# Weighted sums of an attention with the values as the stationary operand, turned back to token rows in the output projection, and sums of squares of the delta norm taken by ACT

## What is computed

```python
def stick_breaking_attention(q, k, v):      # 8 heads of 64
    for blk in range(seq // SB_BLOCK):      # 8 row blocks of 128 tokens
        logits = einsum('bhtd,bhsd->bhts', qh[:, :, start:end], kh[:, :, :end])
        log_remain = where(causal, log_sigmoid(-logits), 0.0)
        log_after = cumsum(log_remain, axis=3, reverse=True) - log_remain
        weights = where(causal, exp(log_sigmoid(logits) + log_after), 0.0)
        outs.append(einsum('bhts,bhsd->bhtd', weights, vh[:, :, :end]))

# in gated_deltanet, o is (seq, 4 heads, 128)
o = rms_norm(o, norm_w) * silu(zf)
# in reference
sb_out = rms_norm(stick_breaking_attention(sb_q, sb_k, sb_v), sb_norm_w[i])
mixed = concatenate([gdn_out, sb_out], axis=-1)
x = x + einsum('bsc,cd->bsd', mixed, w_out[i])
```

## Time and profile before

| | before |
|---|---|
| median of 3 runs | 1545.11 us (1543.13 to 1546.72) |
| the profiled execution | 1548.61 us |
| its span, first to last instruction | 1546.6 us |
| PE busy over the span | 1383.3 us (89%) |
| DVE, ACT, POOL busy | 553.6, 358.9, 257.5 us |
| granted PE clock, mean over the span | 0.957 |
| mixers, from PE's first to its last multiplication | 451.5 to 694.2 us of the span |
| output projection, PE's first transposes to the last route and embed work | 695.3 to about 856 us |

### The profile page before, as it was taken

How to read it: one execution, slowest core, us unless ns; L and a number is a source line. 1 busy time by engine, 2 the same in 40 slices (tenths; PEclk the granted TensorE clock), 3 DMA queues, 4 the chain that set the end, 5 groups by cost and what they waited for, 6 DMA issues and landing times. The chain is left out here.

```text
span 1546.6 us, 16490 instructions
## 1 busy us (share of the span) xinstructions
PE 1383.3 (89%) x5986; PEld 743.0 (48%) x5986; DVE 553.6 (36%) x847; ACT 358.9 (23%) x674; POOL 257.5 (17%) x372
## 2 busy tenths in 40 slices
PE   6999999999999999999999687788778878789997
PEld 4445864444458878874555232232223323234443
DVE  3323024432227887872455221211211111124543
ACT  2221132100036666651212101000000100004322
POOL 1000000110014544532110111111111111111110
PEclk8999999999999999999999899999989999999999
DMA  5212025743422220106214499999999999982231
GB/s 195 68 68 69 14 70 170 196 116 89 141 104 62 65 73 28 29 8 272 81 63 150 173 411 420 421 420 417 418 411 399 404 403 403 402 368 91 82 122 41
DMA packets 107879, 306.96 MB, mean 198 GB/s; under 512 B 22560, under 2 KB 61360, under 8 KB 82096
## 3 DMA queue, kind: packets, MB, share of 16 engines
q1 hardware_dynamic: 98032, 289.42, 49.0%
q0 software_dynamic: 9792, 16.80, 2.9%
HBM read 285.16 MB, written 39.90 MB: 210 GB/s over the span
## 5 line engine op out<-in xcount | busy, mean ns | idle before, releaser
L1620 PE MATMUL pe_gu<-w_gu,xT 128*64 128x512 f32 x1024 | 266.8, 681 | 97.1 <-DMA w_gu<-in_w_expert_up 91.2
L251 PE MATMUL ps<-wide,gst 128*128 128x512 f32 x640 | 285.7, 607 | 3.2 <-DVE wide L404 3.2
L1620 PEld LDWEIGHTS pe_gu<-w_gu,xT 128*64 128x64 f32 x1024 | 82.2, 155 | 259.8 <-issue 257.9
L251 PEld LDWEIGHTS ps<-wide,gst 128*128 128x128 f32 x640 | 123.6, 195 | 155.1 <-issue 153.3
L1824 DVE TENSOR_TENSOR hs<-sg,pe_gu 128x256 f32<-128x256 f32 x32 | 13.5, 421 | 361.0 <-ACT sg L1736 361.0
L1314 PE MATMUL p_x<-wide,pw 128*128 128x512 f32 x256 | 116.4, 608 | 2.1 <-DVE mx L1174 1.4
L1638 PE MATMUL pe_y<-wide,hTe 128*64 128x512 f32 x512 | 115.4, 592 | 1.1 <-DVE ys L1829 1.1
L901 POOL TENSOR_TENSOR wt<-brk,Pm 128x512 f32<-128x512 f32 (+3 forms) x96 | 91.1, 950 | 125.1 <-DVE Pm L827 120.7
L265 PE MATMUL psk<-w_tok,wide 128*128 128x260 f32 (+1 forms) x384 | 111.7, 453 | 0.0
L1709 PE MATMUL pe_y<-w_gu,xT 128*128 128x512 f32 x256 | 111.2, 592 | 0.0
L1560 POOL DMA_INDIRECT y_d<-ys,row_at x32 | 32.5, 1017 | 425.8 <-DVE ys L1829 415.1
(11 more groups left out here) (303 smaller groups left out, 1572.7 us busy)
## 6 DMA issues: line engine op xcount, KB each, us to landing
w_gu<-in_w_expert_gate SPq DMA_DIRECT2D x64, 1024.0 KB, 11.8
w_gu<-in_w_expert_up SPq DMA_DIRECT2D x64, 1024.0 KB, 16.5
wide<-in_w_expert_down SPq DMA_DIRECT2D x64, 1024.0 KB, 19.6
gst<-in_w_in SPq DMA_DIRECT2D x20, 512.0 KB, 4.0
wide_tab<-y_d SPq DMA_DIRECT2D x8, 1024.0 KB, 5.6
qkv_d<-y_sb SPq DMA_DIRECT2D x12, 512.0 KB, 2.6
qk_st<-rows_d SPq DMA_DIRECT2D x8, 768.0 KB, 9.6
gst<-qkv_d SPq DMA_DIRECT2D x8, 768.0 KB, 4.8
```

The lines of the kernel that those rows point to most:

```text
L251: last = pe.matmul(ps[s][:, c], w_ct[:, s, k, :], hT[:, k, c], start=k == 0, stop=k == KT - 1)
L1620: last = pe.matmul(p_gu[e * CAP:(e + 1) * CAP, :], xT[:, s, k, e * CAP:(e + 1) * CAP], wv[:, e, :, k, :], start=k == 0, stop=k == KT - 1)
```

## The change

* Weighted sums: the 64 columns of the values are now the stationary operand and the turned weights (128 columns) the moving one. The two heads of a pair write the upper and the lower 64 partitions of `OB`, so that `OB` holds the result turned: head width by tokens. The sums of both strips of a pair are issued in one group, block by block and head by head, in steps g = 4, 6, 8, ...; there are 48 groups in place of 96. `wT` has a second pair of buffers. The tiles of `mx` that the attention fills are turned, too.
* Output projection: each tile's attention half is first turned back (`turn_back`, 4 transposes into the upper half of `p_m`), ACT takes the squares from there, and DVE's `norm_heads` reads `p_m` and writes the token rows. `turn_back(0)` comes first, `turn_back(1)` after `turn_s(0)` in step 0, and `turn_back(t + 1)` at the start of step t from t = 1. `turn_s` then writes the same part of `p_m`. POOL's root for the delta half of the last tile, DVE's `gated_last` and ACT's squares for them come ahead of the work on tile 1.
* Delta norm: ACT squares head by head, four instructions of 128 columns with an accumulated sum; DVE's `sum` is gone; DVE's `norm` is four instructions of 128 columns with both factors in place of two of 512.
* `scale_w_o` moves from DVE to ACT, at half steps 14 and 22.
* `nsq` and `own` have no memory of their own any more and lie in `w_r` and `ln_row`; so the router weights are loaded after the seventh squares, and `ln_row` after the last scan.
* PE's wait for the memsets stands in the first `ks` piece only.

```diff
--- before.py
+++ after.py
...
         St, Sg = sb("St", [P, GH, P]), sb("Sg", [P, GH, P])
-        nsq = sb("nsq", [P, GW])
+        nsq = w_r[:].rearrange("p k n -> p (k n)")[:, 0:GW]
         nss = sb("nss", [P, GH])
...
         wt = sb("wt", [P, 3, 512])
-        wT = sb("wT", [P, 2, 512])
-        own = sb("own", [P, 512])
+        wT = sb("wT", [P, 2, 2, 512])
+        own = ln_row[:, 0:512]
         GA, GB, GC = (pb(n, [P, GH, P]) for n in ("GA", "GB", "GC"))
...
         PE_AT = {"y1": 0, "xq": 2, "z1": 5, "vt": 7, "y2": 9, "kt": 11, "z2": 13, "ks": 15, "vn": 18, "ods": 21}
-        ACT_AT = {"y1": 0, "xq": 2, "square": 4, "y2": 9, "vn": 18}
-        DVE_AT = {"scale0": 0, "q": 1, "gain": 1, "x": 2, "v": 3, "sum": 3, "k": 5, "xT": 6, "r": 7, "scale1": 8, "norm": 9, "s": 10, "o": 11}
+        ACT_AT = {"y1": 0, "xq": 2, "square": 4, "y2": 9, "scale0": 14, "vn": 18, "scale1": 22}
+        DVE_AT = {"q": 1, "gain": 1, "x": 2, "v": 3, "k": 5, "xT": 6, "r": 7, "norm": 9, "s": 10, "o": 11}
...
                 sp.dma_start(w_o[:], A["w_out"][0].rearrange("(k p) c -> p k c", p=P)).then_inc(wo_in, 16)
-                sp.dma_start(w_r[:, :, 0:NG], A["w_router_group"][0].rearrange("(p k) c -> p k c", k=KT)).then_inc(small_in, 16)
-                sp.dma_start(w_r[:, :, NG:NG + NE], A["w_router_expert"][0].rearrange("(p k) c -> p k c", k=KT)).then_inc(small_in, 16)
                 sp.dma_start(b_r[:, 0:NG], A["b_router_group"][0:1, :].to_broadcast([P, NG])).then_inc(small_in, 16)
                 sp.dma_start(b_r[:, NG:NG + NE], A["b_router_expert"][0:1, :].to_broadcast([P, NE])).then_inc(small_in, 16)
-                sp.dma_start(ln_row[:], A["ln_moe"][0:1, :].to_broadcast([P, D])).then_inc(small_in, 16)
                 for i in range(NT - 2):
...
                     load_z(i + 2)
+                sp.wait_ge(nss_ok, NT - 1)
+                sp.dma_start(w_r[:, :, 0:NG], A["w_router_group"][0].rearrange("(p k) c -> p k c", k=KT)).then_inc(small_in, 16)
+                sp.dma_start(w_r[:, :, NG:NG + NE], A["w_router_expert"][0].rearrange("(p k) c -> p k c", k=KT)).then_inc(small_in, 16)
+                sp.wait_ge(scan_done, G)
+                sp.dma_start(ln_row[:], A["ln_moe"][0:1, :].to_broadcast([P, D])).then_inc(small_in, 16)
...
-                def weighted(g):
-
-                    t, n, c0, c1, e = at(g)
+                def weighted(m):
+
+                    g = 2 * m
+                    t, n, c0, c1, _ = at(g)
                     if g % NS == 0:
                         reach(pe, at_done, g // NS)
-                    pe.wait_ge(ev_done, g + 1)
-                    m = (c1 - c0) // P
-                    h = g // (2 * NS) * 2 + e
-                    for b in range(m):
-                        last = pe.matmul(OB[:, n, e * SD:(e + 1) * SD], wT[:, e, b * P:(b + 1) * P], v_sb[:, c0 // P + b, h * SD:(h + 1) * SD],
-                                         start=g % NS == 0 and b == 0, stop=g % NS == NS - 1 and b == m - 1)
+                    pe.wait_ge(ev_done, g + 2)
+                    nb = (c1 - c0) // P
+                    for b in range(nb):
+                        for e in range(2):
+                            h = g // (2 * NS) * 2 + e
+                            last = pe.matmul(OB[e * SD:(e + 1) * SD, n, :], v_sb[:, c0 // P + b, h * SD:(h + 1) * SD], wT[:, m % 2, e, b * P:(b + 1) * P],
+                                             start=g % NS == 0 and b == 0, stop=g % NS == NS - 2 and b == nb - 1)
                     last.then_inc(pv_done, 1)
...
                     elif piece == "ks":
+                        if i == 0:
+                            pe.wait_ge(setup, 3)
                         for h in range(GH):
...
-                pe.wait_ge(setup, 3)
                 for g in range(G + 3):
...
                         transposes(g - 2)
-                    if g >= 3:
-                        weighted(g - 3)
+                    if g >= 4 and g % 2 == 0:
+                        weighted(g // 2 - 2)
                     if g < G:
...
                     act.wait_ge(tr_done, g + 1)
-                    reach(act, pv_done, g - 1)
-                    act.activation(wT[:, e, 0:m], TB[e][:, 0:m], ACT.Copy).then_inc(ev_done, 1)
+                    reach(act, pv_done, g // 2 - 1)
+                    act.activation(wT[:, g // 2 % 2, e, 0:m], TB[e][:, 0:m], ACT.Copy).then_inc(ev_done, 1)
...
                     c = slice(GW + i // 2 * P, GW + (i // 2 + 1) * P)
-                    act.wait_ge(pv_done, (i + 1) * NS)
+                    act.wait_ge(pv_done, (i + 1) * NS // 2)
                     if i % 2 == 0:
...
+                def scale_w_o(k):
+                    act.wait_ge(wo_in, 16)
+                    act.wait_ge(nw_in, 48)
+                    last = act.activation(w_o[:, k, :], w_o[:, k, :], ACT.Copy, scale=nw[:, k // GH:k // GH + 1])
+                    if k == KT - 1:
+                        last.then_inc(wo_ok, 1)
+
                 def delta(piece, i):
+                    if piece[0:5] == "scale" and 1 <= i <= KT // 2:
+                        scale_w_o(2 * (i - 1) + int(piece[5]))
                     if piece[0] == "y":
...
                         act.wait_ge(O_ok, i)
-                        reach(act, nss_ok, i - 1)
-                        act.activation(nsq[:], mx[:, i - 1, 0:GW], ACT.Square).then_inc(nsq_ok, 1)
+                        reach(act, nm_ok, i - 1)
+                        for h in range(GH):
+                            c = slice(h * GD, (h + 1) * GD)
+                            last = act.activation(nsq[:, c], mx[:, i - 1, c], ACT.Square, accum_out=nss[:, h:h + 1])
+                        last.then_inc(nss_ok, 1)
                     elif piece == "vn":
...
-                def scale_w_o(k):
-                    dve.wait_ge(wo_in, 16)
-                    dve.wait_ge(nw_in, 48)
-                    last = dve.tensor_scalar(w_o[:, k, :], w_o[:, k, :], nw[:, k // GH:k // GH + 1], None, ALU.mult)
-                    if k == KT - 1:
-                        last.then_inc(wo_ok, 1)
-
                 def delta(piece, i):
...
                     b3 = lambda x: x.unsqueeze(2).to_broadcast([P, GH, P])
-                    if piece[0:5] == "scale" and 1 <= i <= KT // 2:
-                        scale_w_o(2 * (i - 1) + int(piece[5]))
-                    elif piece == "q":
+                    if piece == "q":
                         dve.wait_ge(qk_done, i + 1)
...
                         dve.tensor_tensor(mx[:, i, 0:GW], mx[:, i, 0:GW], GC[:].rearrange("p h n -> p (h n)"), ALU.add).then_inc(O_ok, 1)
-                    elif piece == "sum" and i > 0:
-                        dve.wait_ge(nsq_ok, i)
-                        dve.tensor_reduce(nss[:], nsq[:].rearrange("p (h n) -> p h n", h=GH), AX.X, ALU.add).then_inc(nss_ok, 1)
                     elif piece == "norm" and i > 0:
...
                         dve.wait_ge(nrs_ok, i)
-                        dve.tensor_tensor(o.rearrange("p (h n) -> p h n", h=GH), o.rearrange("p (h n) -> p h n", h=GH),
-                                          nss[:].unsqueeze(2).to_broadcast([P, GH, GD]), ALU.mult).then_inc(nz_step, 1)
-                        dve.wait_ge(nz_step, i)
                         dve.wait_ge(z_in[1 - s], 16 * ((i - 1) // 2 + 1))
-                        dve.tensor_tensor(o, o, z_sb[:, 1 - s], ALU.mult).then_inc(nm_ok, 1)
+                        for h in range(GH):
+                            c = slice(h * GD, (h + 1) * GD)
+                            last = dve.scalar_tensor_tensor(o[:, c], o[:, c], nss[:, h:h + 1], z_sb[:, 1 - s, c], ALU.mult, ALU.mult)
+                        last.then_inc(nm_ok, 1)
...
                 def step(t, s, half_t, first, last):
-                    if not last:
-                        heads_rms(t + 1, 1 - s)
                     if first:
...
                         pool.tensor_tensor(gss[:], gss[:], nh[:, 0:GH], ALU.pow).then_inc(gs_ok, 1)
+                    if not last:
+                        heads_rms(t + 1, 1 - s)
+                    if first:
                         constants()
...
                         act.wait_ge(ms_sum, nth)
-                    act.activation(msq[:, s], row(t, slice(GW, None)), ACT.Square).then_inc(msq_ok, 1)
+                    act.wait_ge(back_done, t + 1)
+                    act.activation(msq[:, s], p_m[:, HK:].rearrange("p k n -> p (k n)"), ACT.Square).then_inc(msq_ok, 1)
...
                 copy_g(0, 0)
-                head_squares(1, 1, None)
                 act.activation(hsq[:, 0:GW], row(NT - 1, slice(0, GW)), ACT.Square).then_inc(gsq_ok, 1)
                 copy_s(0, 0)
+                head_squares(1, 1, None)
                 act.wait_ge(gs_sum, 1)
...
                     dve.wait_ge(ms_ok, t + 1)
-                    dve.tensor_tensor(heads(t), heads(t), mss[:, s].unsqueeze(2).to_broadcast([P, SH, SD]), ALU.mult).then_inc(m_ok, 1)
+                    dve.wait_ge(back_done, t + 1)
```

(23 more changed lines are left out.)

6 lines of the change are left out of this document (3 added, 3 removed).

## The result

| | before | after |
|---|---|---|
| median of 14 runs each, on the same chip | 1545.92 us (1538.64 to 1552.9) | 1537.72 us (1529.4 to 1544.46) |
| ratio after to before, 95% interval | | 0.9947 (0.9925 to 0.997) |
| the profiled execution, its span | 1548.61, 1546.6 us | 1542.1, 1540.2 us |
| PE, DVE, ACT, POOL busy over the span | 1383.3, 553.6, 358.9, 257.5 us | 1371.2, 543.5, 371.2, 251.5 us |
| granted PE clock, mean | 0.957 | 0.955 |

A forecast was written before the change was run, and what follows sets the result against it. PE was taken to bound both stages. Mixers -14.9 us (-10.6 - 6.3 + 2) and output projection +10.7 us (0.3 + 5.4 + 2.6 + 2.4) gave -4.2 us: median 1545.1 to 1540.9 us; 80% range 1532 to 1553.

The forecast's parts named there:

- Streaming pair: Weighted sums in the mixers: both halves stream at the same time, 0.115 us per pair, 33.1 us for 288 pairs.
- rival 2: Weighted sums: second half's load lies bare or halves don't overlap at 128 columns; 1570 to 1574 us, chance 0.12.
- Changing the form: Mixers: entering and leaving the divided array costs 0.35 us for each of 48 groups, 16.8 us in all.
- rival 4: Weighted sums: changing the form is nearly free, 0.05 us per group, -14 us more, 1527 us; chance 0.10.
- The wait for `OB`: Mixers, start of each round: PE's 6.8 us wait for ACT's copies is covered by the later first sum, -6.3 us.
- New waits: Mixers: waits behind ACT's squares and scalings, for DVE's scan, POOL's product and PE's transpose; +2 us (0 to +8).
- rival 1: The forecast itself: halves stream together, PE stays the bound, new waits 0 to 6 us; 1535 to 1547 us, chance 0.58.
- DVE and ACT: Mixers: DVE loses about 20 us of 192, to 172; ACT gains 13 of 149, to 162; PE stays the bound.
- `ln_row`: Start of the output projection: its later load lands as PE begins, a tie; +0.3 us (0 to +1.5).
- Step 0: Output projection: PE waits for tile 1's whole chain, 6.8 us where it was 1.84; +5.4 us with 0.5 at the start.
- The clock: Output projection: after 4 us of standing still PE's clock falls again, +2.4 us (0 to +3.3).
- Later steps: Output projection: the turn backs of tiles 2 to 7 stand in full steps, 2.6 us.

The follow-up runs named there:

- e6: The changed kernel with every weighted-sum group of two or more blocks cut in two, over two steps; 1544.55 us, ratio to the kernel before 0.9991.
- e4: The kernel before with only the new delta norm and the scaling of w_o on ACT; 1549.68 us, ratio to the kernel before 1.0032.
- e3: The changed kernel with the delta norm and the scaling of w_o as they were before; 1538.24 us, ratio to the kernel before 0.9942.
- e8: The kernel of e1 plus a third `brk` buffer, with `scale_w_o` back on DVE; 1532.62 us, ratio to the kernel before 0.9914.
- e1: The changed kernel with `turn_back(1)` right after `turn_g(0)`, into the free half of `p_h`, and tile 1 normalised earlier; 1530.52 us, ratio to the kernel before 0.9872.
- e7: The changed kernel with four unused 512-column multiplications ahead of PE's wait in the hole of step 0; 1535.28 us, ratio to the kernel before 0.9929.

## Why the prediction was right, point by point

**The bound.** PE was and is the bound of both stages. Right.

**Streaming pair.** 0.115 us was taken, 0.105 to 0.113 measured. The halves stream side by side at 128 columns, rival 2 is out. The Trainium skill ("TensorE: Matmul & The Clock Gate", Part 3, The mechanism) has the rule that a load runs under a multiplication in flight only where the row groups differ. Both halves share all rows here; by that rule each of the four pairs of a x8 group would show its loads, 0.10 us by the earlier trace rows, and the group would take some 0.98 us in place of 0.58. The row disagrees.

**Changing the form.** 0.35 us was taken, from the logits. By the lines above it is 0.16 within the group, 0.10 to 0.16 ahead and up to 0.1 behind; 0.32 in all for a usual group; e6 gives 0.20 per added spell, whose neighbours are partly the same ones. Summed over the stage, PE's own time went from 231.0 to 214.7 us: weighted sums 61.9 to 37.9, the transposes of the weights 35.2 to 41.2, delta pieces +1.7. That is -16.3, where the prediction had -10.6. The last group is not in these sums; for the other 47, with 280 pairs, 61.9 - 16.3 = 45.6 us remain. At 0.109 us a pair, the middle of the measured ones, the rest, 45.6 - 30.5 = 15.1 us, is 0.32 per spell. So the cost of the form was nearly right, and what the prediction missed (6 us, the last group aside) came from pairs that are a little cheaper than 0.115 (1.7), from a spell cheaper than 0.35 (1.4 over 48), and from old groups that were dearer than 0.105 a record: 61.9 us for 560 records is 0.1105. "Nearly free" (rival 4) was wrong as well. The same skill ("TensorEngine Tiling (Array Packing)", Key Properties) says that a change of tiling mode drains the engine. The direction agrees; it gives no price, and these traces price it at a fifth to a third of a microsecond.

**The wait for `OB`.** -6.3 predicted, and it is gone. Right.

**New waits.** +2 was taken, with 0 to 8 as range; 6.2 us came, plus 1.7 for DVE's state. The range of the sum held, the 0 to 6 of rival 1 didn't, and neither did the value, and the place was wrong: I named the transposes' wait for `wt` (1.2 us, as before), and not the logits' wait for the sigmoids. PE's idle time in the mixers is about what it was (9.7 and 10.6 us): the wait removed was replaced. This miss and the 6 us of PE's own time nearly cancel: -14.9 met the measured -16.3 between the first logits and the last sum partly by luck.

**DVE and ACT.** ACT's busy time was put at 162 us and is 161.7. Each of the four squares leaves a second record, a read of the accumulator, which I hadn't reckoned with. The two kinds overlap, though: from the first square to ACT's next instruction 1.17 us pass, where it was 0.52 (e4 has the same), so the 1.3 taken was nearly right. DVE fell by 10.0 us, not 20: the four fused products take 19.1 us, as much as the two products that they replace (19.7), where I had them at the price of the second alone, and only the sum (4.7) and `scale_w_o` (5.8) are gone. These are the squares and their reads, the fused products, and DVE's other products of the same kind and shape (least, median and most ns of one):

```profile
L803 ACT ACTIVATE w_r<-mx 128x128 f32<-128x128 f32 x28 | 8.2, 306 | 0.0
L803 ACT ACTIVATION_READ_ACCUMULATOR w_r<-mx 128x1 f32 x28 | 5.5, 198 | 0.0
...
L890 DVE SCALAR_TENSOR_TENSOR mx<-mx,nss,z_sb x28: 339/660/1361, 502.0 to 670.7; 128x128 f32<-128x128 f32 x28
...
L872 DVE SCALAR_TENSOR_TENSOR Rr<-GA,coef,vb x32: 319/335/336, 469.4 to 667.1; 128x128 f32<-128x128 f32 x32
```

The price of a fused product is not one number. In 11 of the 28 POOL is idle all the while, and each of these takes 0.34 us; the 17 that run beside an instruction of POOL take 0.66 to 1.36. At 0.34 all 28 would take 9.5 us, near the 9.1 that I had. L872, which reads `GA` in PSUM, takes no more than 0.34 though POOL runs beside it. So the step that failed is the price of DVE's products beside POOL; that POOL is the cause is argued from this alone, and no run changed POOL's list. On the end it hardly shows, since neither engine sets the pace (e3, e8: about 2 us).

**`ln_row`.** +0.3 us was taken for a tie. Its load is issued at 674.88 and lands 3.5 us later, 1.3 us before PE begins at 679.68, after the same 1.17 us as before: nothing is paid.

**Step 0.** The chain of tile 1 was put at 6.8 us from `turn_s(0)` to the end of `turn_s(1)`. The terms written there add up to 7.3, so 6.8 was a slip; `turn_back(1)` came after 1.28 us and not 1.9, which made up for it. The rows give 698.36 - 691.37 = 6.99, of which 0.45 is the clock. The hole of 3.7 us and its releaser were as described. e1 shows that the order made it.

**The clock.** +2.4 us was taken for a second spell of 3.2 us at its worst; e7 puts it at 1.5 in the profiled execution, and the three others with the hole have 1.4 to 2.8. In part it was offset by a shorter first spell, 0.7, which is the luck of the execution.

**Later steps.** 2.6 us for the six turn backs. From DVE's first addition to `x` to its last the change added 2.3, and this is the same in all eight kernels with the changed output projection (123.1 us against 120.8). The other 1.3 of the 3.6 lies behind it, up to POOL's copy, where the executions differ by as much: 20.5 and 21.3 us with the projection as before, 20.5 to 21.8 with the changed one. Four records of the last embedding multiplication ran at half clock after the change (3.58 us in place of 1.88) and in e3 (3.46), in no other. That is an accident of the execution, and little of it reaches POOL's copy: in e1 and e6, without it, the copy comes after 21.3 and 21.4 us, as in e3.

**Sum.** Mixers and wait -16.9, output projection +10.1 (10.7 predicted), -6.8 in the stages that the change touches, where -4.2 was predicted. Rival 1 held: PE is the bound, both halves stream together, and the hole in step 0 is there. The medians differ by 8.2 us, twice the forecast; by the interval the change is worth 4.6 to 11.6 us, so -4.2 lies just outside it. PE's own time in the mixers is the term that was too small.

## What to carry to other kernels

When short multiplications use half of the array's columns, put the two halves next to each other in one group and make the groups as long as buffers allow: the streaming pays per record, the change of form per group. An operand that comes out turned has to be turned back, and that step should go into a space that is free early, not into the one that a later step must first clear (6.2 us here by e1, more than the rest of the stage cost). Work moved to ACT is free only where nobody waits for what stands behind it in ACT's list (e4: 4.5 us). Before two executions are compared stage by stage, look at the granted clock of the stage in both (1.6 us here, in six of ten).

## What the runs showed of the hardware that I had not expected

* Two halves of the columns overlap even when their records don't alternate: groups of four records and four records of the other half take 0.59 us, as alternating ones do (0.58); with eight and eight it is 1.51 against 1.03, and the second half starts with the fifth record of the first.
* The granted clock fell at the end of the 3.7 us of idle time, from 2.4 to 1.2 GHz (after the change): 0.97 over the 6.08 us that end with the hole, 0.50 in the 0.91 behind it, 0.87 in the next 7.94. Four multiplications that nobody reads kept the clock at 1.00 (e7).
* A square of 128 columns with accumulation leaves two records on ACT, of 0.306 and 0.198 us, which overlap: four of them take 1.17 us up to the next instruction, against 0.52 for a plain square of 512 columns.
* On DVE, a fused product of 128 columns with its inputs in SBUF took 0.34 us while POOL was idle, and 0.66 to 1.36 us beside POOL's instructions; a plain product of 512 columns (L882) took 1.06 to 1.70 in the mixers of the kernel before.
